# Where the first two output products of a merge are begun, and which banks a recurrence uses

## The chip, the cores and the metric

The kernel runs on one core of one Trainium2 chip. The metric is the device time of one execution in microseconds (us), the median of several runs. TensorE (PE in the rows) does the matrix products into PSUM, which has eight banks of 128 x 512 fp32 numbers; PEld is its weight load; VectorE is DVE, ScalarE is ACT, GpSimd is POOL, and SyncE (SP) issues the transfers from memory.

## The reference, cut to what matters

Two layers of a first block are computed, then two layers of a second block, on 512 tokens of width 1024, all in fp32. A layer of the first block is:

```python
proj = rmsnorm(x, norm_w[l]) @ w_in[l]          # q, k, v, gates, z and gate_a, gate_b
y_a = gated_delta_branch(q_a, k_a, v_a, ab_a, z_a, ...)     # 8 heads, both directions
y_b = diff_attention_branch(q_b, k_b, v_b, z_b, ...)        # 8 heads
merged = (jax.nn.sigmoid(gate_a) * (y_a @ w_pa[l])
          + jax.nn.sigmoid(gate_b) * (y_b @ w_pb[l]))
x = x + merged @ w_out[l]
```

The second block (window attention, gated attention, an mLSTM and a feed-forward part) isn't touched by the change.

## The kernel before, in words

Everything lies transposed in SBUF: a matrix of 512 tokens x 1024 is eight tiles (K-tiles) of 128 x 512. A product of one 128-column tile of a weight is eight K-steps, and each K-step is three matmuls of 128x128 by 128x512 (high part by high part, high by low, low by high; lines L309, L312, L313, in `Stream.product`), since each fp32 operand is split into two parts of the faster type fp32r. So a product is 24 matmuls into one bank.

A phase is a `Block`: all engines start it together and its end is a barrier. A layer runs delta_phase, merge_phase (a), diff_phase, merge_phase (b), out_phase. A merge has eight output tiles. Output tile n is `sigmoid(h @ gate tile) * (y @ weight tile)`, and its two products use the two halves of one weight chunk of 1 MB. The half 0 products (gates, from `hT`) go to banks 0 and 1, the half 1 products (outputs, from `yS`) to banks 2 and 3. The chunks (i, c), with i from 0 to 3 and c 0 or 1, are a `Stream`:

- `load` (L219) is issued on SP into `raw[c]`. SP issues chunk (i+1, c) when chunk (i, c) has been split (`load_after`, called from `run_sync`). The delta and diff phases issue the merge's chunks (0, 0) and (0, 1) themselves and no more: chunk (1, 0) and (1, 1) are the first thing that SP issues in the merge phase. In the second layer's merge (b), 832 KB of constants are issued on SP ahead of them (the argument `pairs`).
- `high` (ACT, L260) and then `low` (DVE, L266) split a chunk from `raw` into the slot `ws[c]`. Both wait for the load and for `slot_free`, which the first matmul of a product raises that was built with `frees`: when PE begins with one slot, the other is free.
- PE waits in `ready` for both parts.

The last head of delta and the last heads of diff have no further projections to compute. PE there takes work from a generator (`fill`, taken in pieces by `some(fill, n)` and emptied by `drain(fill)`). Its last part is `first_gates`: the two half 0 products of the merge's chunks (0, 0) and (0, 1). The merge phase then begins on PE with the two half 1 products of these chunks, 48 matmuls, and continues with chunk (1, 0).

In the last head of delta the recurrence over four chunks (s = 0 to 3) runs in two directions d: PE forms k by the state (`ks`, L1548, bank AB+d = 4 and 5), DVE forms r, PE forms y (L1555, bank YB+d = 6 and 7), ACT copies it out as v_new (L1730), PE forms the state's product (L1568, bank AB+d) and the outputs (L1579, L1581, bank 3). After s = 3 ACT squares the outputs (L1668), DVE normalises them (L1820), PE transposes them (`turn_out`, L1454), DVE gates them (L1825), ACT and DVE write the high and low parts of `yS` (L1677, L1831), and the phase ends. The end of diff has the same chain: PE forms the last output (L2126), ACT squares (L2190), DVE normalises (L2264), PE transposes (`turn_out`, L2097), DVE gates (L2273), ACT and DVE write the parts (L2197, L2279).

Of the kernel before, what the change touches and what calls it, by code (L numbers as in the profile page):

```python
# [10 lines left out]
ALU = mybir.AluOpType  # L11
# [3 lines left out]
P = 128  # L15
# [11 lines left out]
HEADS = 8  # L27
# [321 lines left out]
def whole(gen):  # L349
    for last in gen:  # L350
        pass
    return last
# [322 lines left out]
        yield  # L675


def first_outputs(k, pe, st, banks, x, steps, ready):

    st.credit(pe)  # L680
    st.ready(pe, 0, 0)
    halves = [st.product(pe, k.bank[banks[h]][:, :], 0, h, x, steps=steps, end=False) for h in range(2)]
    for t in steps:
        ready(t)
        for part in halves:
            next(part)
            yield


def merge_phase(k, st, following, yS, macc, mS, pairs=()):  # L690

    nc = k.nc
    st.open()
    tile, sig, mul, step, hi, loaded = k.sems("tile_ready", "sigmoid_ready", "merged_ready", "merge_step", "merged_high_done",
                                              "constants_loaded")
    with ExitStack() as ctx:
        room = Carve(k.cb[:, :], F32)
        sg, mt = room(2, SEQ), room(2, SEQ)

        with nc.Block() as block:  # L700
            @block.gpsimd
            def _(pool):
                k.clear_old(pool)

            @block.sync
            def _(sp):
                for dst, src in pairs:
                    sp.dma_start(dst, src).then_inc(loaded, 16)
                st.run_sync(sp, following)
                sp.wait_ge(loaded, 16 * len(pairs))  # L710

            @block.tensor
            def _(pe):
                pe.sem_inc(tile, 1)
                for c in range(2):
                    st.ready(pe, 0, c)
                    whole(st.product(pe, k.bank[2 + c][:, :], c, 1, yS, frees=c == 1)).then_inc(tile, 2 - c)

                with pe.Fori(1, KT // 2) as i:
                    for c in range(2):  # L720
                        st.ready(pe, i, c)

                        pe.wait_ge(mul, nth(i, 2, c))
                        whole(st.product(pe, k.bank[c][:, :], c, 0, k.hT)).then_inc(tile, 1)
                        whole(st.product(pe, k.bank[2 + c][:, :], c, 1, yS)).then_inc(tile, 1)
                if mS is not None:

                    pe.wait_ge(mul, 2 + KT - 1)
                    drain(first_outputs(k, pe, following, OUT_BANKS_MERGE, mS, MERGE_FIRST, lambda t: pe.wait_ge(mul, 3 + t)))

            @block.scalar
            def _(act):
                def body(i, c, last):
                    act.wait_ge(tile, nth(i, 4, 2 * c))
                    act.activation(sg[:, c], k.bank[c][:, :], ACT.Sigmoid).then_inc(sig, 1)
                    if mS is not None:
                        act.wait_ge(step, nth(i, 4, 2 * c + 1))
                        act.activation(mS[:, 0, bass.ds(i * 2 + c, 1)], mt[:, c:c + 1], ACT.Copy).then_inc(hi, 1)
                pipelined(act, KT // 2, 2, lambda i, c: st.high(act, i, c), body, lambda: following.first_high(act, st),
                          handed=True)  # L740
                if mS is not None:
                    following.second_high(act)

            @block.vector
            def _(dve):
                chain = Chain(dve, step)

                dve.sem_inc(mul, 2)

                def body(i, c, last):  # L750
                    n = i * 2 + c
                    dve.wait_ge(sig, nth(i, 2, c))
                    dve.wait_ge(tile, nth(i, 4, 2 * c + 1))
                    if mS is None:
                        dve.tensor_tensor(macc[:, bass.ds(n, 1)], sg[:, c:c + 1], k.bank[2 + c][:, :].rearrange("p (o n) -> p o n", o=1),
                                          ALU.mult).then_inc(mul, 1)
                    else:
                        chain.at(i, 4, 2 * c)
                        chain(dve.tensor_tensor(mt[:, c], sg[:, c], k.bank[2 + c][:, :], ALU.mult))
                        chain(dve.tensor_tensor(mt[:, c:c + 1], mt[:, c:c + 1], macc[:, bass.ds(n, 1)], ALU.add))  # L760
                        dve.wait_ge(hi, nth(i, 2, c))
                        dve.tensor_tensor(mS[:, 1, bass.ds(n, 1)], mt[:, c:c + 1], mS[:, 0, bass.ds(n, 1)].bitcast(F32),
                                          ALU.subtract).then_inc(mul, 1)
                pipelined(dve, KT // 2, 2, lambda i, c: st.low(dve, i, c), body, lambda: following.first_low(dve, st),
                          handed=True)
                if mS is not None:
                    following.second_low(dve)
                dve.wait_ge(mul, 2 + KT)
    k.next_phase()


OUT_BANKS_MERGE, OUT_BANKS_ATT = (0, 2, 1, 3), (0, 1, 2, 3)
MERGE_FIRST = tuple(range(KT - 1))

# [395 lines left out]
def delta_phase(k, st, following, l, pA, cg, tab, lam, yS, wsp):  # L1170
# [23 lines left out]
    with ExitStack() as ctx:  # L1194
# [74 lines left out]
        with nc.Block() as block:  # L1269
# [123 lines left out]
            def _(pe):  # L1393
# [22 lines left out]
                def gates_ahead():  # L1416

                    for x, step in enumerate(first_gates(k, pe, following, taken, 4 * HEADS)):
                        yield
                        if x == KT - 1:  # L1420
                            for _ in range(KT):
                                yield

                def scratch(name, core):
                    use = scratch_use(name, core)
# [71 lines left out]
                def core(i, p, first=False, ahead=2):  # L1497
# [41 lines left out]
                    for s in range(NS):  # L1539
# [11 lines left out]
                        for d in range(2):  # L1551
                            c = chunk(d, s)
                            if s > 0:
                                pe.wait_ge(r_ready, nth(i, 2 * (NS - 1), 2 * (s - 1) + d))
                            pe.matmul(B[YB + d][:, 0:P], Xf[:, d, c], tmv[:, c] if s == 0 else r[:, d], start=True, stop=True).then_inc(y_ready, 1)  # L1555
                        if s == 1 and ahead:
                            turn_k(i + 1, 1 - p, i)
                        if s == 2 and ahead:
# [26 lines left out]
                            some(fill, 2 if s == 2 else 1)  # L1585
                    if ahead:
                        gram(i + 1, 1 - p, q, YB)
                    drain(fill)

                st.ready(pe, 0, 0)  # L1590
                for last in first_chunk(st, pe, (B[0][:, :], B[1][:, :]), k.hT, norm.ready(pe), gates.product(pe)):
# [15 lines left out]
                gram(0, 0, kk[:, 0], YB + 1)  # L1607
                gram(0, 0, q, YB)
                cores(core)
                turn_out(HEADS - 1, HEADS - 1, "out")  # L1610

            @block.scalar
            def _(act):
# [69 lines left out]
                def core(i, p, first=False, ahead=2):  # L1683
# [42 lines left out]
                    for s in range(NS):  # L1726
                        for d in range(2):
                            c = d * NS + chunk(d, s)
                            act.wait_ge(y_ready, nth(i, 2 * NS, 2 * s + d))
                            act.activation(vn[:, d], B[YB + d][:, 0:P], ACT.Copy, scale=small(p, BP + c, 1)).then_inc(vn_ready, 1)  # L1730
                        if not ahead:
                            continue
                        if s == 0:
                            silu(i + 1, 1 - p, 1)
                        elif s == 1:
                            token_squares(i + 1, 1 - p, 1, i)
                            copy_k(i + 1, i)
                            if ahead > 1:
                                st.high(act, i + 2, 1)
                        elif s == 2:  # L1740
                            silu(i + 1, 1 - p, 2)
                            token_squares(i + 1, 1 - p, 0, i)
                            act.preload_act_table_set(LN_EXP)
                            if ahead > 1:
                                pad_copy(i + 2, 0)
# [239 lines left out]
def diff_phase(k, st, following, lam, yS):  # L1985
# [22 lines left out]
    with ExitStack() as ctx:  # L2008
# [17 lines left out]
        with nc.Block() as block:  # L2026
# [38 lines left out]
            def _(pe):  # L2065
                st.credit(pe)

                def stream():
# [12 lines left out]
                    for _ in first_gates(k, pe, following, taken, 4 * HEADS):  # L2081
                        yield
                        yield

                def turn_v(h):
                    pe.wait_ge(raw_ready, nth(h, 3, 2))
# [50 lines left out]
                for u in range(UNITS1):  # L2137
# [9 lines left out]
                        output(u - 1)  # L2147
                    some(fill, KT)
                output(UNITS1 - 1)
                drain(fill)  # L2150
                turn_out(HEADS - 1)

            @block.scalar
            def _(act):
# [952 lines left out]
def build(nc, a, out):  # L3107
    ctx = ExitStack()
    with ctx:
# [22 lines left out]
        with ExitStack() as one:  # L3132
# [10 lines left out]
            for l in range(DEPTH):  # L3143
# [3 lines left out]
                delta_phase(k, s_delta, s_ma, l, pA, cg, tab, lam, yS, split)  # L3147
                with ExitStack() as two:
                    macc = k.sb(two, "macc", [P, KT, SEQ], F32)
                    merge_phase(k, s_ma, s_diff, yS, macc, None)  # L3150
                    diff_phase(k, s_diff, s_mb, lam, yS)
                    with ExitStack() as three:
                        mS = k.sb(three, "mS", [P, 2, KT, SEQ], F32R)
                        merge_phase(k, s_mb, s_out, yS, macc, mS, () if more else [(k.cb[:, CB_CAUS:CB_N], a["cb"][:, CB_CAUS:CB_N])])
                        out_phase(k, s_out, s_next, mS, macc[:, 0:2], OUT_BANKS_MERGE, KT - 1, [(pA[:, :], a["pA"][l + 1])] if more else (),
                                  weights(split, a["gA"], l + 1) if more else None)
        with ExitStack() as one:
# [66 lines left out]
```

## Time and profile before

| what | us |
| --- | --- |
| median of 3 runs (3218.54 to 3222.21) | 3218.66 |
| the profiled execution, its own time | 3222.45 |
| its span in the profile | 3220.7 |
| PE busy, of the span | 3033.8 |
| end of delta's last DVE work to merge (a), first layer | 462.52 to 463.37 |
| end of diff's last DVE work to merge (b), first layer | 827.90 to 828.74 |

The profile times each instruction of one execution on each engine, from the span's start. A line of a timeline has the start, the duration, the engine, the source line, the operation with its output and inputs, a count if several are merged, and in brackets the idle time of the engine before it with what ended it. Matmuls overlap each other in the records, so the pace of a run of them is read from the distance of their starts.

### The profile page before, as it was taken

Reading aid. Unit: us, or ns where it says so; the run is one execution under the profiler, and the core shown is the slowest. Engines: PE = TensorE matmul, PEld = TensorE weight load, DVE = VectorE, ACT = ScalarE, POOL = GpSimd, SP = SyncE. Lnnn points to the kernel's source line nnn. Section 1 sums busy time; section 2 is a strip of 40 time slices with the busy share of each in tenths; the row PEclk is TensorE's granted clock in tenths of the full one; section 3 lists DMA queues with packets and bytes.
Section 4 is the critical chain, followed back from the end, with each engine's and each line's share of the span. In section 5 each row is a group of like instructions: output and inputs, shape, how many; then the busy total and the mean of one; then the engine's idle time right before and its main releaser. Section 6 shows DMA issues by size and latency. Waiting matters only on the chain. (4 is left out here: it accounts for less than half of the span.)

```text
span 3220.7 us, 55034 instructions
## 1 busy us (share of the span) xinstructions
PE 3033.8 (94%) x22250; PEld 2393.4 (74%) x22250; DVE 1701.3 (53%) x2532; ACT 1456.3 (45%) x2841; POOL 418.3 (13%) x276
## 2 busy tenths in 40 slices
PE   7999989999898999899999989989999999899998
PEld 4777767777776777777776867767888777678887
DVE  5777742566446777724665435544333445443343
ACT  4455532555334555523555245643333356543332
POOL 1544510000013455400000010001000100010000
PEclk9999999999999999999999999989999999999999
DMA  3211112221222112022221222112222221022222
GB/s 130 74 61 61 61 49 92 70 70 56 83 91 80 61 63 78 28 79 82 69 71 61 83 93 82 40 40 92 101 95 91 79 82 53 4 102 95 101 91 79
DMA packets 39723, 239.34 MB, mean 74 GB/s; under 512 B 6352, under 2 KB 6992, under 8 KB 13904
## 3 DMA queue, kind: packets, MB, share of 16 engines
q1 hardware_dynamic: 39504, 236.27, 21.4%
q8 instruction: 156, 2.56, 0.3%
q14 instruction: 63, 0.52, 0.1%
HBM read 229.36 MB, written 2.16 MB: 72 GB/s over the span
## 5 line engine op out<-in xcount | busy, mean ns | idle before, releaser
L309 PE MATMUL bank<-hT,ws 128*128 128x512 f32 x2112 | 877.4, 415 | 53.9 <-DVE hT L500 26.2
L313 PE MATMUL bank<-hT,ws 128*128 128x512 f32 x2112 | 831.5, 394 | 0.0
L312 PE MATMUL bank<-hT,ws 128*128 128x512 f32 x2112 | 830.4, 393 | 1.0 <-issue 1.0
L309 PEld LDWEIGHTS bank<-hT,ws 128*128 128x128 f32 x2112 | 400.9, 190 | 145.6 <-issue 66.2
L266 DVE TENSOR_TENSOR ws<-raw,ws 128x2048 fp32r<-128x2048 f32 x160 | 367.6, 2298 | 216.1 <-ACT ws L260 213.4
L260 ACT ACTIVATE ws<-raw 128x2048 fp32r<-128x2048 f32 x172 | 328.8, 1911 | 327.8 <-PE bank L309 204.5
L313 PEld LDWEIGHTS bank<-hT,ws 128*128 128x128 f32 x2112 | 399.6, 189 | 89.7 <-issue 1.6
L312 PEld LDWEIGHTS bank<-hT,ws 128*128 128x128 f32 x2112 | 401.9, 190 | 69.5 <-issue 1.4
L917 PE MATMUL bank<-uS,ws 128*128 128x512 f32 x512 | 201.8, 394 | 0.0
L921 PE MATMUL bank<-uS,ws 128*128 128x512 f32 x512 | 201.2, 393 | 0.0
L920 PE MATMUL bank<-uS,ws 128*128 128x512 f32 x512 | 200.3, 391 | 0.0
L1796 DVE SCALAR_TENSOR_TENSOR cb<-cb,cw 128x512 f32<-128x512 f32 x192 | 177.9, 927 | 4.7
L309 PE MATMUL bank<-yS,ws 128*128 128x512 f32 x384 | 160.0, 417 | 20.8 <-PEq L1269 6.2
L313 PE MATMUL bank<-yS,ws 128*128 128x512 f32 x384 | 157.8, 411 | 0.0
L312 PE MATMUL bank<-yS,ws 128*128 128x512 f32 x384 | 157.7, 411 | 0.0
L455 POOL TENSOR_TENSOR sq<-sq 128x512 f32<-128x512 f32 x18 | 35.1, 1950 | 926.6 <-ACT sq L444 926.6
L1000 DVE TENSOR_TENSOR uS<-u,uS 128x512 fp32r<-128x512 f32 x64 | 44.3, 693 | 206.4 <-ACT uS L983 206.4
L1004 DVE TENSOR_TENSOR xT<-xT,bank 128x512 f32<-128x512 f32 x128 | 87.9, 687 | 121.7 <-PE bank L921 121.1
L2184 ACT ACTIVATE pr<-bank,sc 128x512 f32<-128x512 f32 x128 | 86.6, 682 | 140.8 <-DVE sc L2250 140.8
L2250 DVE TENSOR_REDUCE sc<-bank 128x1 f32<-128x512 f32 x128 | 82.3, 685 | 119.2 <-PE bank L2108 119.2
L455 POOL TENSOR_TENSOR macc<-macc 128x512 f32<-128x512 f32 x12 | 25.3, 2106 | 787.1 <-ACT macc L444 787.1
L979 ACT ACTIVATE u<-bank 128x512 f32<-128x512 f32 x64 | 38.3, 599 | 181.1 <-PE bank L313 181.1
(361 smaller groups left out, 4903.7 us busy)
## 6 DMA issues: line engine op xcount, KB each, us to landing
raw<-in_w_ff SPq DMA_DIRECT2D x64, 1024.0 KB, 4.9
raw<-in_w_delta SPq DMA_DIRECT2D x32, 1024.0 KB, 4.9
raw<-in_w_diff SPq DMA_DIRECT2D x32, 1024.0 KB, 4.9
raw<-in_w_att SPq DMA_DIRECT2D x20, 1024.0 KB, 4.9
raw<-in_w_merge_a SPq DMA_DIRECT2D x16, 1024.0 KB, 4.9
raw<-in_w_merge_b SPq DMA_DIRECT2D x16, 1024.0 KB, 5.0
raw<-in_w_out SPq DMA_DIRECT2D x16, 1024.0 KB, 5.0
rows<-sum_rows SPq DMA_DIRECT2D x16, 512.0 KB, 6.1
```

The costliest lines, as they stand in the source:

```text
L260: act.activation(self.k.ws[:, c % 2, 0], self.k.raw[:, c % 2], ACT.Copy).then_inc(self.high_done, 1)
L266: dve.tensor_tensor(self.k.ws[:, c % 2, 1], self.k.raw[:, c % 2], self.k.ws[:, c % 2, 0].bitcast(F32), ALU.subtract).then_inc(self.low_don ...
L309: first = pe.matmul(out, hi, x[:, 0, k], start=(begin and k == steps[0]), stop=False)
L312: pe.matmul(out, hi, x[:, 1, k], start=False, stop=False)
L313: last = pe.matmul(out, lo, x[:, 0, k], start=False, stop=(end and k == steps[-1]))
L917: first = pe.matmul(o, hi, uS[:, 0, kk], start=(kk == 0), stop=False)
L920: pe.matmul(o, hi, uS[:, 1, kk], start=False, stop=False)
L921: last = pe.matmul(o, lo, uS[:, 0, kk], start=False, stop=(kk == 3))
L1004: dve.tensor_tensor(k.xT[:, n], k.xT[:, n], k.bank[4 + n % 4][:, :], ALU.add).then_inc(added, 1)
L1796: ins = dve.scalar_tensor_tensor(cv[:, j], pad[:, j, w:w + SEQ], cw[:, j, w:w + 1], cv[:, j], ALU.mult, ALU.add)
L2184: act.activation(pr[:, u % 2, m], B[SB + m][:, :], ACT.Exp, bias=sc[:, u % 2, m:m + 1], accum_out=sc[:, u % 2, 2 + m:3 + m]).then_inc(p_re ...
L2250: dve.tensor_reduce(sc[:, u % 2, m:m + 1], B[SB + m][:, :], AX_X, ALU.max, negate=True).then_inc(max_ready, 1)
```

## The change

Seven of the eight K-steps of each of the two half 1 products of chunks (0, 0) and (0, 1) are issued in the phase before, as the last part of the same generator (`first_merges`): in delta's last head into banks 6 and 7, in diff's into banks 4 and 5. The merge phase then issues the eighth K-step of each, three matmuls, and reads these banks for its first two output tiles. `frees` stays at the first matmul that the merge phase issues for chunk (0, 1). The transposes at the end of both phases are issued with steps of the generator ahead of them and behind them: four ahead and the rest behind in delta, six ahead and the rest behind in diff. The recurrence's product y moves, in all eight heads, from the first 128 columns of banks 6 and 7 to columns 256 to 383 of banks 4 and 5, whose first 128 columns hold `ks` and the state's product.

```diff
+def first_merges(k, pe, st, banks, x, ready):
+
+    halves = [st.product(pe, k.bank[b][:, :], c, 1, x, frees=False, steps=MERGE_FIRST, end=False) for c, b in enumerate(banks)]
+    for t in MERGE_FIRST:
+        ready(t)
+        for part in halves:
+            next(part)
+            yield
...
-def merge_phase(k, st, following, yS, macc, mS, pairs=()):
+def merge_phase(k, st, following, yS, macc, mS, begun, pairs=()):
...
-                    whole(st.product(pe, k.bank[2 + c][:, :], c, 1, yS, frees=c == 1)).then_inc(tile, 2 - c)
+                    whole(st.product(pe, k.bank[begun[c]][:, :], c, 1, yS, frees=c == 1, steps=(KT - 1,), begin=False)).then_inc(tile, 2 - c)
...
+                    merged = k.bank[begun[c] if isinstance(i, int) and i == 0 else 2 + c][:, :]
...
+MERGE_DELTA, MERGE_DIFF = (6, 7), (4, 5)
 OUT_BANKS_MERGE, OUT_BANKS_ATT = (0, 2, 1, 3), (0, 1, 2, 3)
 MERGE_FIRST = tuple(range(KT - 1))
...
+                    yield from first_merges(k, pe, following, MERGE_DELTA, yS, lambda t: pe.wait_ge(ylo_ready, t + 1))
...
-                            pe.matmul(B[YB + d][:, 0:P], Xf[:, d, c], tmv[:, c] if s == 0 else r[:, d], start=True, stop=True).then_inc(y_ready, 1)
+                            pe.matmul(B[AB + d][:, QUAD:QUAD + P], Xf[:, d, c], tmv[:, c] if s == 0 else r[:, d], start=True, stop=True).then_inc(y_ready, 1)
...
-                    drain(fill)
+                        drain(fill)
+                    else:
+                        some(fill, 4)
+                        turn_out(i, i, "out")
+                        drain(fill)
...
-                turn_out(HEADS - 1, HEADS - 1, "out")
...
-                            act.activation(vn[:, d], B[YB + d][:, 0:P], ACT.Copy, scale=small(p, BP + c, 1)).then_inc(vn_ready, 1)
+                            act.activation(vn[:, d], B[AB + d][:, QUAD:QUAD + P], ACT.Copy, scale=small(p, BP + c, 1)).then_inc(vn_ready, 1)
...
+                    pe.wait_ge(p_ready, 2 * UNITS1)
+                    yield from first_merges(k, pe, following, MERGE_DIFF, yS, lambda t: pe.wait_ge(ylo, t + 1))
...
                 output(UNITS1 - 1)
+                some(fill, 6)
+                turn_out(HEADS - 1)
                 drain(fill)
-                turn_out(HEADS - 1)
```

## Rows read from the trace of the kernel before

**Rows 1.** The page's part 1: busy time and share of the span.
```profile
PE 3033.8 (94%) x22250; PEld 2393.4 (74%) x22250; DVE 1701.3 (53%) x2532; ACT 1456.3 (45%) x2841; POOL 418.3 (13%) x276
```

**Rows 2.** Timeline of the end of diff, first layer.
```profile
821.00 1.05 PE L2126 MATMUL bank<-vtm,AT 128*128 128x128 f32 x8
...
825.01 0.66 PE L2097 MATMUL bank<-cc,O 128*128 128x128 f32 x4 [2.95 <-DVE O L2264]
...
827.21 0.69 DVE L2279 TENSOR_TENSOR yS<-yt,yS 128x512 fp32r<-128x512 f32 x1 [0.75 <-ACT yS L2197]
...
828.74 0.77 PE L309 MATMUL bank<-yS,ws 128*128 128x512 f32 x1 [3.07 <-PEq L2026]
```

**Rows 3.** Timeline of the end of delta, first layer, and SP's first issue in merge (a).
```profile
459.17 1.11 PE L1454 MATMUL bank<-cc,o 128*128 128x128 f32 x4 [2.63 <-DVE o L1820]
...
461.83 0.69 DVE L1831 TENSOR_TENSOR yS<-tmv,yS 128x512 fp32r<-128x512 f32 x1 [0.76 <-ACT yS L1677]
...
463.37 0.76 PE L309 MATMUL bank<-yS,ws 128*128 128x512 f32 x1 [3.09 <-PEq L1269]
...
463.86 1.95 SPq L219 DMA_DIRECT2D raw<-in_w_merge_a  x2
```

**Rows 4.** Busy time by stretch: PE's count and granted clock, PEclk (1.00 is 2.4 GHz).
```profile
463.30:467.70 4.40, 4.33 (x10) 3.47 (x11) 0.00 (x0) 1.62 (x2) 0.00 (x0) 0.50 0.68 214
467.70:472.00 4.30, 4.30 (x19) 3.46 (x18) 0.56 (x1) 0.34 (x1) 0.00 (x0) 0.96 0.71 269
822.00:825.00 3.00, 0.06 (x1) 0.00 (x0) 0.69 (x1) 1.98 (x10) 0.00 (x0) 1.00 0.00 0
```

**Rows 5.** Timeline of merge (a), first layer: how chunk (1, 0) becomes ready.
```profile
471.66 1.92 ACT L260 ACTIVATE ws<-raw 128x2048 fp32r<-128x2048 f32 x1 [6.72 <-PE bank L309]
...
473.71 2.29 DVE L266 TENSOR_TENSOR ws<-raw,ws 128x2048 fp32r<-128x2048 f32 x1 [1.58 <-ACT ws L260]
...
476.76 0.40 PE L309 MATMUL bank<-hT,ws 128*128 128x512 f32 x1
```

**Rows 6.** Timelines: PE begins chunk (1, 0) in the other three merges.
```profile
843.15 0.47 PE L309 MATMUL bank<-hT,ws 128*128 128x512 f32 x1 [0.92 <-issue]
...
1411.47 0.40 PE L309 MATMUL bank<-hT,ws 128*128 128x512 f32 x1
...
1778.36 0.47 PE L309 MATMUL bank<-hT,ws 128*128 128x512 f32 x1 [0.92 <-issue]
```

**Rows 7.** Timelines of SP: chunks (1, 0), (1, 1) issued in those three.
```profile
828.80 1.01 SPq L219 DMA_DIRECT2D raw<-in_w_merge_b  x2
...
1397.67 1.02 SPq L219 DMA_DIRECT2D raw<-in_w_merge_a  x2
...
1764.33 1.02 SPq L219 DMA_DIRECT2D raw<-in_w_merge_b  x2
```

**Rows 8.** DMA issues, chunk (1, 0) alone, four merges in time: us to landing.
```profile
raw<-in_w_merge_a SPq DMA_DIRECT2D x1, 1024.0 KB, 5.0
...
raw<-in_w_merge_b SPq DMA_DIRECT2D x1, 1024.0 KB, 5.1
...
raw<-in_w_merge_a SPq DMA_DIRECT2D x1, 1024.0 KB, 4.9
...
raw<-in_w_merge_b SPq DMA_DIRECT2D x1, 1024.0 KB, 6.2
```

**Rows 9.** Timeline of the recurrence: s = 0 with, s = 2 without a step between.
```profile
443.71 0.60 PE L1555 MATMUL bank<-tmv,Xf 128*128 128x128 f32 x4
...
444.85 0.60 PE L1568 MATMUL bank<-XT,kd 128*128 128x128 f32 x4
...
450.79 0.75 PE L1555 MATMUL bank<-XT,Xf 128*128 128x128 f32 x4 [0.29 <-DVE XT L1914]
...
451.74 0.75 PE L1568 MATMUL bank<-XT,kd 128*128 128x128 f32 x4 [0.20 <-ACT XT L1730]
```

More of the change, by code:

```diff
@@ L754, in body @@
                     if mS is None:
-                        dve.tensor_tensor(macc[:, bass.ds(n, 1)], sg[:, c:c + 1], k.bank[2 + c][:, :].rearrange("p (o n) -> p o n", o=1),
+                        dve.tensor_tensor(macc[:, bass.ds(n, 1)], sg[:, c:c + 1], merged.rearrange("p (o n) -> p o n", o=1),
                                           ALU.mult).then_inc(mul, 1)
@@ L758, in body @@
                         chain.at(i, 4, 2 * c)
-                        chain(dve.tensor_tensor(mt[:, c], sg[:, c], k.bank[2 + c][:, :], ALU.mult))
+                        chain(dve.tensor_tensor(mt[:, c], sg[:, c], merged, ALU.mult))
                         chain(dve.tensor_tensor(mt[:, c:c + 1], mt[:, c:c + 1], macc[:, bass.ds(n, 1)], ALU.add))
@@ L3149, in build @@
                     macc = k.sb(two, "macc", [P, KT, SEQ], F32)
-                    merge_phase(k, s_ma, s_diff, yS, macc, None)
+                    merge_phase(k, s_ma, s_diff, yS, macc, None, MERGE_DELTA)
                     diff_phase(k, s_diff, s_mb, lam, yS)
@@ L3153, in build @@
                         mS = k.sb(three, "mS", [P, 2, KT, SEQ], F32R)
-                        merge_phase(k, s_mb, s_out, yS, macc, mS, () if more else [(k.cb[:, CB_CAUS:CB_N], a["cb"][:, CB_CAUS:CB_N])])
+                        merge_phase(k, s_mb, s_out, yS, macc, mS, MERGE_DIFF, () if more else [(k.cb[:, CB_CAUS:CB_N], a["cb"][:, CB_CAUS:CB_N])])
                         out_phase(k, s_out, s_next, mS, macc[:, 0:2], OUT_BANKS_MERGE, KT - 1, [(pA[:, :], a["pA"][l + 1])] if more else (),
```

## Prediction, made before the change was run

> **What bounds the kernel.** The page comes first: PE is busy for 3033.8 us, 94% of the span [rows 1], and no other engine for more than 53%, so only PE's idle time, or PE's own work at a lower clock, can be saved. The timelines of the two kinds of phase end show where PE is idle. At the end of diff PE issues the last output at 821.00, is next busy at 825.01 after 2.95 us of idleness, and then idle for 3.07 us until the merge starts at 828.74 [rows 2]. At the end of delta it is idle for 2.63 us and for 3.09 us [rows 3]. There are four such ends (two layers), with some 6 us each. The view by stretches shows a second cost: the merge's first ten matmuls run in 4.4 us at a granted clock of 0.50 (1.2 GHz), the following nineteen in 4.3 us at 0.96 [rows 4]. So the reader sees two things that filling the end could save: idle time, and ten matmuls at 0.44 us in place of 0.23.
>
> The third thing to look at is what PE needs next. In merge (a) ACT begins to split chunk (1, 0) at 471.66, DVE at 473.71, and PE begins with the chunk at 476.76 [rows 5]. ACT had waited 6.72 us for a PE matmul, the one that frees the slot; the load had been issued at 463.86 [rows 3] and landed after 5.0 us [rows 8], at 468.9, and was hidden under the 48 matmuls. These are exactly the matmuls that the change takes away from behind it.
>
> **The moved matmuls.** Seven K-steps of two products are 14 steps, 42 matmuls. At 0.233 us each (nearest row: 19 in 4.30 us, 0.226, with clock 0.96 [rows 4]; the K-step of three is taken as 0.70 us) they are 9.8 us in each phase end. What is left in the merge is 6 matmuls, 1.4 us.
>
> **The end of delta.** By the order in the code, of the 14 steps one stands after the outputs of s = 1, two inside s = 2, two after it, two inside s = 3, four ahead of the transpose and three behind. Three stand where PE waits for nothing: 3 x 0.70 = 2.1 us on the chain. Those inside stand partly in waits: from y to the state's product it takes 1.14 us with a step between and 0.95 us without [rows 9], so 0.19 us; the same inside the pair of ks and y I put at 0.14, twice; the last stands in the wait for v_new and costs nothing. The outputs are late by 2.1 + 0.19 + 0.28 = 2.6 us. The four steps behind them, 2.8 us, cover ACT's squares and DVE's normalisation, which take about as long (PE's idle 2.63 us [rows 3]); if that cover were longer than the wait, each 0.1 us would be paid. The transpose gains: 1.11 us at the low clock [rows 3] against 0.66 us in diff [rows 2], 0.45 us. The three behind it, 2.1 us, end before the chain through DVE and ACT does (from 459.17 + 1.11 to 462.52, 2.2 us). So the merge starts 2.1 us later.
>
> **The end of diff.** The generator's calls count out so that four steps of `first_merges` stand ahead of the last output (L2126): 2.8 us. The output then issues for 0.9 us, six steps follow, 4.2 us, against a normalised output that comes 4.0 us after the output's start (821.00 to 825.01 [rows 2]): PE arrives 5.1 us after it, 1.1 us late. The transpose is thus at 825.01 + 3.9 = 828.9. Four steps behind it, 0.45 + 2.8 us, end at 832.2, DVE's last at 831.8 (2.9 us after the transpose, as 825.01 to 827.90). With PE last and its pipe to empty, and the 0.84 us from there to the merge, it starts at 833.1 instead of 828.74: 4.4 us later (bounds 3.9 and 4.6).
>
> **What is late next.** SP isn't changed: it issues chunk (1, 0) when the merge phase begins. PE has 1.4 us of work then. The chunk needs its landing, then 2.05 us from ACT's start to DVE's, 2.29 us of DVE [rows 5], and 0.1 us to PE: landing plus 4.45 us. For the second merges the order on ACT and DVE (first tile's sigmoid and sum ahead of the split) is done before the load lands, so it adds nothing. Queued behind PE's wait are all of the merge's remaining products, in order; ACT and DVE have nothing but this chunk. With SP's times [rows 3, 7], shifted by the start's delay, and the landings of the same transfers [rows 8]:
>
> - merge (a), layer 1: 463.86 + 2.1 + 5.0 + 4.45 = 475.4, before 476.76 [rows 5]: 1.35 earlier.
> - merge (a), layer 2: 1397.67 + 2.1 + 4.9 + 4.45 = 1409.1, before 1411.47 [rows 6]: 2.35 earlier.
> - merge (b), layer 1: 828.80 + 4.4 + 5.1 + 4.45 = 842.75, before 843.15 [rows 6]: 0.4 earlier.
> - merge (b), layer 2: 1764.33 + 4.4 + 6.2 + 4.45 = 1779.4, before 1778.36 [rows 6]: 1.0 later (here the constants are in front).
>
> Together 3.1 us are gained. The waits are about 8 us in each merge: the 48 matmuls filled the time of a load, and what the change saves in the phase end it gives back there.
>
> **The clock after that wait.** The merge's start in rows 4 shows what PE's idleness of 3.07 to 3.09 us after little work does: clock 0.50 for ten matmuls, 4.4 us. A wait of 8 us after six matmuls should do no less. Ten to twelve matmuls of chunk (1, 0) at 0.427 instead of 0.23 us cost 1.95 to 2.35 us, taken as 2.15, in each of four merges: 8.6 us. This replaces the low clock at the merge's start, whose end is already in the comparison. The Trainium skill ("TensorE: Matmul & The Clock Gate", section "HAM oscillation — how this bites in real kernels") describes this pattern: bursts of matmuls with a longer wait for a transfer between them each start at the low clock again. By that rule the change pays 8.6 us; if the trace's exception counted (822 to 825, 3 us nearly without work at clock 1.00 [rows 4]) it would pay nothing.
>
> **The moved banks.** The product y goes to the bank of ks and the state's product. In program order each of these is read before the other is written, by the same semaphores as before, so no wait is added. There are 128 products y (eight heads, four s, two d, two layers). The rows show the products to the one bank and to the other at the same 0.60 us when nothing is waited for [rows 9], equal within the 0.01 us of the record; so the bound is 128 x 0.01 = 1.3 us either way, and I take zero. The new waits in `first_merges` (low parts of heads 0 to 6, last exponentials) are fulfilled when PE arrives.
>
> **The sum.** -3.1 + 8.6 = +5.5 us. Against the profiled execution's own 3222.45 (span 3220.7 and 1.75 around it) that is 3228.0; this execution lies 3.8 us above the median of 3218.66, and the forecast for the median is 3224.2. A measurement of this kernel tells about 0.2% (6.4 us) from no change, so this is "no change", on the slow side of it.
>
> **Rivals.**
>
> *The load lands later.* Its price is the landing, one to one, as it ends the wait. Rows 8 show 4.9 to 6.2 us. Were all at 6.2, three merges lose 1.2 + 1.1 + 1.3 = 3.6 us more: +9.1, 3227.8, slower. It decides from 0.3 us more in each of three merges. For it: in the changed kernel two loads of 1 MB are issued in the same way, and the fourth landing shows how much it varies. Against it: three of four agree within 0.2 us. Chance 0.2.
>
> *The clock stays high through the wait.* Then -3.1 us, 3215.6, no change. For it the three microseconds at 1.00 [rows 4], against it the length of the wait. Chance 0.1.
>
> *The load is hidden anyway.* If chunk (1, 0) were there when PE wants it, the merges would go from their start to chunk (1, 0) in 1.4 us instead of 13.4 to 14.4 us: 12.0 to 13.0 less 2.1 or 4.4 of delay, near 9.9, 8.6, 10.3 and 8.6 us, about -37 us, 3181, faster. It needs SP to issue that load before the phase; the code and rows 3 and 7 have it at the start each time. Chance 0.07, for what I have overlooked.
>
> *The forecast*, with its own range 3220 to 3228: 0.63.
>
> **Chances.** Faster by over 0.2%: the hidden load and a remainder, 0.10. Slower: the later load, 0.2, and the upper third of the forecast's own range, 0.2: 0.40. Within 0.2%: 0.50. The range for 8 in 10 is 3215 to 3232: from the clock that stays high to a later load with twelve slow matmuls each; the hidden load stays outside.
>
> **What the changed profile would show.** Merge starts later by 2.1 and 4.4 us after the last output or recurrence step of the phase before; PE's two idle gaps at the phase ends gone, but for the barrier's 0.8 to 1 us; six matmuls of `yS` at 0.23 us at the merge's start; then 7 to 8.5 us of idleness that DVE's L266 ends, with ACT's L260 released by a DMA instead of a matmul; then some ten matmuls at 0.43 us. Wrong would be a wait under 5 us, matmuls at full pace behind it, or a start of the merge that moved by under 1 or over 6 us.

## The result, and the profile after

| kernel | median, us | executions | ratio to before | 95% interval |
| --- | --- | --- | --- | --- |
| before, beside it | 3218.54 | 13 | 1 | |
| changed | 3226.36 (3221.11 to 3232.26) | 13 | 1.0026 | 1.0019 to 1.0033 |
| changed, once more, beside a before of 3219.79 | 3226.93 | 11 | 1.0019 | 1.0010 to 1.0028 |

The changed kernel is 8.4 us slower by the first ratio (0.0026 x 3218.5; interval 6.1 to 10.6 us) and 6.1 us by the second (3.2 to 9.0 us), where 5.5 us slower was forecast. The forecast had set 0.2% as the bound of "no change" and gave "no change" a chance of 0.50, "slower" 0.40. The first ratio lies a little beyond that bound, the second just within it.

The profiled execution of the changed kernel is the fastest of its 13 (3221.11 us, span 3219.3), so its span says little by itself; its stages do. The changed kernel has other line numbers: there L1467 and L2115 are the transposes that were L1454 and L2097, and L2144 is the last output of diff, before L2126. First the start of merge (a) of the first layer, timeline of PE and ACT, with the lines that answer to [rows 3, 5]. This execution runs 1.92 us ahead of the profile of before at that point (SP issues its last chunk ahead of it at 368.33 instead of 370.25).

```profile
460.14 0.66 PE L1467 MATMUL bank<-cc,o 128*128 128x128 f32 x4
...
463.88 0.47 PE L309 MATMUL bank<-yS,ws 128*128 128x512 f32 x1 [0.99 <-PEq L1281]
...
469.35 1.91 ACT L260 ACTIVATE ws<-raw 128x2048 fp32r<-128x2048 f32 x1 [3.91 <-DMA raw<-in_w_merge_a]
...
471.40 2.29 DVE L266 TENSOR_TENSOR ws<-raw,ws 128x2048 fp32r<-128x2048 f32 x1 [5.24 <-ACT ws L260]
...
473.79 0.77 PE L309 MATMUL bank<-hT,ws 128*128 128x512 f32 x1 [8.27 <-DVE ws L266]
474.36 0.63 PE L312 MATMUL bank<-hT,ws 128*128 128x512 f32 x1
```

The reader is to see four things. The two idle gaps of [rows 3] are gone: the transpose has no idle time in front and takes 0.66 us instead of 1.11, and the merge starts after 0.99 us of idleness instead of 3.09. In their place PE is idle for 8.27 us before chunk (1, 0), and what ended it is DVE's part of the split. And ACT's idle time before that split was ended by a DMA, where it was a matmul in [rows 5]. Last, PE's records are then 0.63 us long and 0.42 us apart: the low clock. The view by stretches of the same kernel gives it in numbers (columns as in [rows 4]):

```profile
463.90:465.50 1.60, 1.60 (x6) 1.00 (x6) 0.03 (x1) 1.53 (x2) 0.00 (x0) 1.00 0.36 51
465.50:473.70 8.20, 0.02 (x1) 0.00 (x0) 2.96 (x3) 2.40 (x2) 0.00 (x0) 0.78 0.63 247
473.70:476.90 3.20, 3.11 (x7) 2.48 (x8) 0.88 (x2) 1.91 (x1) 0.00 (x0) 0.50 0.49 148
476.90:481.00 4.10, 4.10 (x19) 3.39 (x18) 2.00 (x1) 0.00 (x0) 0.00 (x0) 0.99 0.54 176
```

Six matmuls at clock 1.00, a wait in which the clock falls, seven at 0.50, then full speed. The other three merges, timeline of PE, which answer to [rows 6]:

```profile
840.88 0.77 PE L309 MATMUL bank<-hT,ws 128*128 128x512 f32 x1 [7.73 <-DVE ws L266]
...
1405.39 0.77 PE L309 MATMUL bank<-hT,ws 128*128 128x512 f32 x1 [7.71 <-DVE ws L266]
...
1775.05 0.77 PE L309 MATMUL bank<-hT,ws 128*128 128x512 f32 x1 [9.68 <-DVE ws L266]
```

PE's waits sum to a line that the kernel before doesn't have:

```profile
PE bank L309 <- DVE ws L266: 33.4, 4, 9.7
```

The end of diff, first layer (this execution is 1.36 us ahead there), answers to [rows 2]:

```profile
822.42 1.05 PE L2144 MATMUL bank<-vtm,AT 128*128 128x128 f32 x8
...
827.51 0.60 PE L2115 MATMUL bank<-cc,O 128*128 128x128 f32 x4
...
831.51 0.48 PE L309 MATMUL bank<-yS,ws 128*128 128x512 f32 x1 [0.59 <-PEq L2042]
```

Less the 1.36 us, the last output is 2.78 us later than before, the transpose 3.86, the merge's start 4.13.

### The profile page after: what moved, and what is told of

Same layout as the page of the kernel before. It is cut to its first block and busy times, and to the rows that moved or that the text cites. A ratio compares the mean times of both kernels' runs of the same rounds, so it can differ in the third digit from the quotient of the medians.

```text
span 3219.3 us, 55036 instructions
## 1 busy us (share of the span) xinstructions
PE 3024.6 (94%) x22250; PEld 2386.5 (74%) x22250; DVE 1703.6 (53%) x2532; ACT 1456.5 (45%) x2841; POOL 417.2 (13%) x276
## 5 line engine op out<-in xcount | busy, mean ns | idle before, releaser
L309 PE MATMUL bank<-hT,ws 128*128 128x512 f32 x2112 | 880.3, 417 | 85.5 <-DVE ws L266 33.4
L309 PEld LDWEIGHTS bank<-hT,ws 128*128 128x128 f32 x2112 | 402.4, 191 | 178.5 <-issue 98.5
L266 DVE TENSOR_TENSOR ws<-raw,ws 128x2048 fp32r<-128x2048 f32 x160 | 367.7, 2298 | 229.2 <-ACT ws L260 226.6
L309 PE MATMUL bank<-yS,ws 128*128 128x512 f32 x384 | 157.6, 410 | 11.5 <-issue 4.4
L312 PE MATMUL bank<-yS,ws 128*128 128x512 f32 x384 | 154.5, 402 | 0.0
L313 PE MATMUL bank<-yS,ws 128*128 128x512 f32 x384 | 154.4, 402 | 0.0
```

Of the source, the lines that this page charges most:

```text
L266: dve.tensor_tensor(self.k.ws[:, c % 2, 1], self.k.raw[:, c % 2], self.k.ws[:, c % 2, 0].bitcast(F32), ALU.subtract).then_inc(self.low_don ...
L309: first = pe.matmul(out, hi, x[:, 0, k], start=(begin and k == steps[0]), stop=False)
L312: pe.matmul(out, hi, x[:, 1, k], start=False, stop=False)
L313: last = pe.matmul(out, lo, x[:, 0, k], start=False, stop=(end and k == steps[-1]))
```

## The experiments

Each experiment is compared with executions of the kernel before on the same chip. The intervals are those of the ratio, and "us on before" is the ratio less one, times the median of before. It differs from the difference of the two medians by up to 1.5 us, and by 3.4 us for e10. e7, e10 and e11 have five executions each, the others 11 or 12.

One number more is used, the "four merges". In a profile, take the distance from a mark in or ahead of the last head of the phase before a merge to a mark at the next phase's start, less the same distance in the profile of before, and add up the four. The marks are ACT's table loads at 396.12 and 566.54, 801.93 and 970.90, 1329.10 and 1501.68, 1737.12 and 1894.05 us of before. This sum leaves out what wanders elsewhere, but it is one execution each. For the changed kernel it is +0.56, +1.33, -1.88 and +3.74, together +3.75, and +4.21 in its second profile. Three kernels that have all 48 matmuls in each merge, as before, give +1.93 (e1), +1.91 (e6) and +1.56 (e12). So the profile of before is itself about 1.8 us on the quick side there, and 1.8 us are to be taken off each of these sums.

**The moved banks alone (e1).**

```diff
-pe.matmul(B[YB + d][:, 0:P], Xf[:, d, c], ...)
+pe.matmul(B[AB + d][:, QUAD:QUAD + P], Xf[:, d, c], ...)
-act.activation(vn[:, d], B[YB + d][:, 0:P], ...)
+act.activation(vn[:, d], B[AB + d][:, QUAD:QUAD + P], ...)
```

> The kernel before, with nothing of the change but the recurrence's product y in banks 4 and 5. Theory (the moved banks cost nothing): the time of before, 3218.5 us, within 2 us. Rival (the shared bank costs something, spread over 16 heads): part of the 8 us that the change lost shows up here, 2 to 8 us slower.

Measured: 3220.79 us, ratio 1.0000 (0.9991 to 1.0008). The moved banks cost nothing that can be measured: zero, with 2.9 us either way.

**One phase end alone (e2, e3).** Only the steps of one phase are begun early; the other merge issues its two products whole, in banks 2 and 3.

```diff
-MERGE_DELTA, MERGE_DIFF = (6, 7), (4, 5)
+MERGE_DELTA, MERGE_DIFF = (6, 7), (2, 3)        # e2; e3: (2, 3), (4, 5)
-                    yield from first_merges(k, pe, following, MERGE_DIFF, yS, ...)     # e2; e3: the one in delta
```

> The change without its part in diff: merge (b) begins as before. Theory: two of four waits are left. The start of chunk (1, 0) is 1.35 and 2.35 us earlier, two stretches at the low clock cost 4.3 us: +0.6 us on before. Rival (the loss sits in the end of delta, or in the moved banks): most of +8 us.

> The change without the K-steps in delta: merge (a) begins as before; y's banks stay moved. Theory: -0.4 and +1.0 us for the start of chunk (1, 0), 4.3 us for the clock: +4.9 us on before. Rival (loss in delta): no difference from before.

Measured: e2 3220.60 us, ratio 1.0001 (0.9992 to 1.0009), +0.3 us; e3 3223.05 us, ratio 1.0011 (1.0002 to 1.0019), +3.5 us. The expectations were +0.6 and +4.9. By the ratios the diff part carries the larger loss, as the sum had it, but the two intervals overlap, and the four merges of the two profiles (+5.44 and +4.69) have it the other way round. So which end costs more isn't settled; e2's interval ends at +2.9 us, so the end of delta alone doesn't carry the loss. The two add to 3.8 us, 2 to 5 us short of what the whole shows; the intervals are wide enough for that. Where the steps of a phase stay in place, the merge behind it begins with 7 to 13 slow matmuls as before, and where they are moved, a wait of 7.7 to 9.4 us with 7 to 12 slow matmuls behind it appears.

**The clock in the wait (e4, e8).** Extra matmuls, results unused, keep PE at work in the wait.

```diff
+                for _ in range(DUMMIES):            # 30 in e4, 36 in e8
+                    pe.matmul(k.bank[4 if mS is None else 6][:, :], k.hT[:, 0, 0, 0:P], k.hT[:, 0, 0], start=True, stop=True)
+
                 with pe.Fori(1, KT // 2) as i:
```

> The changed kernel with 30 extra matmuls (128x128 by 128x512, results unused, in a free bank) between the two last K-steps and chunk (1, 0) of each merge, 7 us of work inside a wait of 7.7 to 9.7 us. Theory (the clock that falls in the wait costs 2.15 us in each merge): the waits stay, the matmuls behind them run at 0.23 us each, and the time falls by 8.6 us against the changed kernel's 3226.4, to about 3218. Rival (the loss is in the wait and the clock plays no part): no difference from the changed kernel, 3226.

> As the run with 30 extra matmuls, with 36 (8.4 us of work), which left 1.3 to 2.8 us of idleness and the clock high in two merges of four. Theory: the clock stays high in all four, the start of chunk (1, 0) moves by under 0.3 us: 7 to 8.6 us faster than the changed kernel, at most 1 us from before. Rival: as with 30, +3.5 us on before.

With 30, the timeline of PE shows the clock kept in the first two merges and lost in the two others, where the remaining idle time was longest (in the third after one matmul at full pace; its load landed after 6.5 us, where it took 4.8 in the changed kernel). The starts of chunk (1, 0), and in the last two a record behind it:

```profile
474.04 0.47 PE L309 MATMUL bank<-hT,ws 128*128 128x512 f32 x1 [1.32 <-issue]
...
840.44 0.47 PE L309 MATMUL bank<-hT,ws 128*128 128x512 f32 x1 [1.69 <-issue]
...
1405.44 0.47 PE L309 MATMUL bank<-hT,ws 128*128 128x512 f32 x1 [2.52 <-issue]
...
1406.11 0.63 PE L313 MATMUL bank<-hT,ws 128*128 128x512 f32 x1
...
1774.81 0.76 PE L309 MATMUL bank<-hT,ws 128*128 128x512 f32 x1 [2.79 <-issue]
1775.37 0.63 PE L312 MATMUL bank<-hT,ws 128*128 128x512 f32 x1
```

It measured 3222.37 us, ratio 1.0011 (1.0002 to 1.0020): +3.5 us on before, where the expectation had all four merges at full speed and the time of before. With 36, no matmul of chunk (1, 0) is slow in any merge. Its starts:

```profile
477.20 0.47 PE L309 MATMUL bank<-hT,ws 128*128 128x512 f32 x1
...
843.09 0.40 PE L309 MATMUL bank<-hT,ws 128*128 128x512 f32 x1
...
1407.52 0.47 PE L309 MATMUL bank<-hT,ws 128*128 128x512 f32 x1 [0.86 <-issue]
...
1775.79 0.47 PE L309 MATMUL bank<-hT,ws 128*128 128x512 f32 x1 [1.66 <-issue]
```

In the first layer's merge (a), which starts at 467.28 here, the view of stretches has the extra matmuls and the start of chunk (1, 0) at clock 1.00:

```profile
464.00:474.00 10.00, 9.01 (x41) 7.09 (x39) 2.13 (x3) 3.76 (x4) 0.00 (x0) 1.00 0.50 191
474.00:478.00 4.00, 3.91 (x18) 2.95 (x17) 2.89 (x2) 1.45 (x3) 0.00 (x0) 1.00 0.12 49
```

It measured 3219.04 us, ratio 0.9997 (0.9988 to 1.0006): 1.0 us faster than before. Against the changed kernel's +8.4 and +6.1 us that is 9.4 and 7.1 us, where 8.6 was forecast. By the four merges it is less: -0.52 against +3.75 and +4.21, so 4.3 and 4.7 us. Of the difference 1.3 us is known. In the third merge the load of chunk (1, 0) landed after 6.2 us instead of 4.8, and the chunk began 10.7 us after the merge's start instead of 9.4, a start that had been expected to move by under 0.3 us; in the other three it moved by 0.0 to 0.3.

So more matmuls, with nothing else altered, take the loss away. The clock is its cause, and without it the change is worth about nothing (-1.0 us, with 2.9 us either way): the idle time of the phase end is only moved.

**The load earlier (e5, e6).** SP issues the chunks (1, 0) and (1, 1) as its last work in the phase before. In the first layer that is far ahead: at 415.07 us in e5, where the merge starts at 462.89. e5 is the changed kernel with it, e6 and e12 (the same kernel again) the kernel before.

```diff
+    def second_loads(self, sp):
+        for c in range(2):
+            self.load_after(sp, 0, c)
...
-            with sp.Fori(0, self.N - 1) as i:
+            with sp.Fori(done, self.N - 1) as i:           # done = 1 in the merges
...
+                following.second_loads(sp)                 # last on SP in delta and in diff
```

> The changed kernel with the loads of the merge's chunks (1, 0) and (1, 1) issued by SP at the end of the phase before (as soon as (0, 0) and (0, 1) are split) instead of at the merge's start. Theory (the wait is for this load, then for the split): the landing falls out of the wait. Merge (a): the split starts when the slot is free, 0.8 us after the start, and chunk (1, 0) begins near 5.2 us after it instead of 9.9 and 9.4; merge (b): ACT is busy with the first tile until 3.7 us, so near 8.0 instead of 9.4 and 11.3. Sum -13.5 us against the changed kernel, so 5 us faster than before; the low clock is still paid in most merges. Rival (the wait is for something else, slot or banks): no difference from the changed kernel.

> The kernel before with the same earlier loads, nothing else. Theory: before, the load was hidden under 48 matmuls and the slot was what ACT waited for, so no difference, within 2 us. Rival (the load mattered already): faster by over 3 us.

> The kernel before with the earlier loads, once more: it came out 5.5 us slower than before, where no difference was expected, with no stage of its profile slower where the loads moved. If that was the spread between groups of executions: within 3 us of before. If the earlier loads cost something real: again 4 us or more.

In e5 the wait shrinks as the load leaves it. Timeline of PE, first layer (the kernels with earlier loads have five lines more ahead of these, so L314 and L271 are L309 and L266):

```profile
462.89 0.47 PE L314 MATMUL bank<-yS,ws 128*128 128x512 f32 x1 [0.99 <-PEq L1286]
...
468.77 0.61 PE L314 MATMUL bank<-hT,ws 128*128 128x512 f32 x1 [4.24 <-DVE ws L271]
...
836.19 0.77 PE L314 MATMUL bank<-hT,ws 128*128 128x512 f32 x1 [6.36 <-DVE ws L271]
```

Chunk (1, 0) of merge (a) begins 5.9 us after the start instead of 9.9 (5.2 had been expected: ACT began the split only 1.45 us after the start, at 464.34, behind its first sigmoid). Merge (b) begins it after 8.0 us, as expected. So the load was what PE waited for. The four starts of the chunk come 12.2 us earlier in sum, of 13.5 expected. It measured 3218.88 us, ratio 0.9993 (0.9984 to 1.0002), -2.3 us on before: 8 to 11 us better than the changed kernel. The low clock is still paid: behind the waits of 4.2 and 6.4 us there are 8, 11, 7 and 14 slow matmuls, no fewer than in the changed kernel.

e6 missed: 3224.70 us, ratio 1.0017 (1.0008 to 1.0026), +5.5 us where zero was expected. e12 was to tell chance from cost and speaks for a cost: 3223.29 us, ratio 1.0013 (1.0003 to 1.0024), +4.2 us. It isn't in the four merges of their profiles (+1.91 and +1.56, as in e1). Where it goes isn't settled: e6's profile is level with that of before at 1894 us, and its 2.2 us of longer span lie behind that, where nothing was changed. Something of 4 us that the earlier loads cost may also lie in e5, e7 and e11.

**Fewer steps moved (e7, e10, e11).** Only the first of the two products is begun early, 21 matmuls, and its steps stand where PE waits anyway: none ahead of diff's last output, none behind the outputs of s = 1 and s = 2 in delta. The merge keeps 27 matmuls to hide the split behind. e7 has the earlier loads, e10 hasn't, e11 is e7 with three K-steps of the second product more in delta, one ahead of the transpose and two behind it.

```diff
-    halves = [st.product(pe, k.bank[b][:, :], c, 1, x, frees=False, steps=MERGE_FIRST, end=False) for c, b in enumerate(banks)]
+    part = st.product(pe, k.bank[banks[0]][:, :], 0, 1, x, frees=False, steps=MERGE_FIRST, end=False)
...
-                    whole(st.product(pe, k.bank[begun[c]][:, :], c, 1, yS, frees=c == 1, steps=(KT - 1,), begin=False)).then_inc(tile, 2 - c)
+                    left = (KT - 1,) if c == 0 else tuple(range(KT))
+                    whole(st.product(pe, k.bank[begun[c]][:, :], c, 1, yS, frees=c == 1, steps=left, begin=c == 1)).then_inc(tile, 2 - c)
...
-                some(fill, 6)
+                some(fill, 4)
                 turn_out(HEADS - 1)
```

> Only the first of the two products is begun in the phase before (7 K-steps, 4.9 us), put where PE waits anyway (two inside s = 2, two inside s = 3 and three ahead of the transpose in delta; four ahead and three behind it in diff, none ahead of the last output), with the earlier loads. The merge keeps 27 matmuls, 6.3 us, with the slot free after 0.7 us. Theory: chunk (1, 0) is ready 5.2 us (a) and 8.0 us (b) after the start, so PE waits 0 and 1.7 us, the clock stays high, the start moves by less than 0.5 us: 7.1 and 6.4 us saved in each merge, 27 us faster than before. Rival (saving at the phase end is always given back): within 6 us of before.

> As the run that begins only the first product, but with the loads at the merge's start as in before. Theory (the wait is the load's): chunk (1, 0) is ready 9.5 us after the start, PE's 27 matmuls take 6.3 us (8.7 with a low clock at the start), so it waits 1 to 3 us; against before the start of chunk (1, 0) is 4 us earlier in (a), 3.4 to 4.7 us in (b): 12 to 16 us faster than before, less up to 4 us where the clock falls. It tells how much of the 18 us of that run was the earlier load.

> As the run that begins only the first product with earlier loads, and in delta three K-steps of the second product more, issued behind the transpose. There that run left 3.2 us of idleness at the end of delta and began the merge with 13 slow matmuls. Theory: the gap shrinks to 1.1 us, the merge starts at the high clock, 18 matmuls are left there, and chunk (1, 0) begins 5.2 us after the start instead of 9.0: 3.8 us less in each of two merges, 7.6 us, so 25 us faster than before. Rival (the split is ready later, or the clock falls all the same): within 3 us of that run.

| run | median, us | ratio (95% interval) | us on before | by the medians | expected | four merges |
| --- | --- | --- | --- | --- | --- | --- |
| e10 | 3210.31 | 0.9960 (0.9946 to 0.9973) | -12.9 | -9.5 | -12 to -16, less up to 4 | -6.4 |
| e7 | 3203.55 | 0.9944 (0.9930 to 0.9958) | -18.0 | -16.5 | -27 | -16.6 |
| e11 | 3198.11 | 0.9933 (0.9919 to 0.9946) | -21.6 | -21.7 | -25 | -25.1 |

All three beat both kernels, with the same idea and half to seven tenths of the steps. e10 shows that fewer steps gain without the earlier loads too. The order among the three is that of the medians, but the intervals of neighbours overlap. e10's four waits ahead of chunk (1, 0) are 2.0 to 4.5 us, with slow matmuls behind three of them. In e7 the miss is in merge (a): PE is idle for 3.18 us ahead of it in the first layer, as in before, and its first 13 matmuls run at 0.50 (in the second layer 3.07 us and seven):

```profile
462.00:465.80 3.80, 0.66 (x4) 0.42 (x4) 1.44 (x2) 1.00 (x2) 0.00 (x0) 0.87 0.00 0
465.80:471.50 5.70, 5.64 (x13) 4.46 (x14) 2.14 (x2) 3.91 (x4) 0.00 (x0) 0.50 0.00 1
```

In e11 the same place has 1.69 us of idleness and no low clock, and chunk (1, 0) begins 5.9 us after the start:

```profile
462.34 0.47 PE L314 MATMUL bank<-yS,ws 128*128 128x512 f32 x1 [1.69 <-PEq L1296]
...
468.23 0.47 PE L314 MATMUL bank<-hT,ws 128*128 128x512 f32 x1 [1.46 <-issue]
```

The step from e7 to e11 is 3.6 us by the ratios and 8.5 by the four merges, against 7.6 expected. By the times alone it isn't clear of noise; that the gap, the low clock and the later start of chunk (1, 0) are gone, in both layers, is what the traces show.

**The changed kernel once more (e9).**

> The changed kernel as it is, once more, for a second profile and a second ratio. Theory: +5.5 us on before by the sum of the terms, up to +8 as first measured; the four waits before chunk (1, 0) at 7.7 to 9.7 us with 7 to 13 slow matmuls behind each. Rival (the first ratio was a lucky or unlucky draw): within 2 us of before.

Measured: ratio 1.0019, as in the table at the top. Its waits are 8.31, 7.73, 7.86 and 9.74 us (33.6 in sum, 33.4 in the first profile), with 7, 10, 10 and 6 slow matmuls of chunk (1, 0) behind them, against 7, 10, 7 and 13 in the first. The waits repeat; how long the clock stays down behind them repeats in the first layer only.

## Why the prediction was right, step by step

*The moved matmuls.* Right: six at the high clock in 1.6 us where the merge began with ten at the low one.

*The end of delta.* Forecast 2.1 us later; measured 463.88 against 463.37 less 1.92, 2.43 us. In the second layer the start came only 0.8 us later in the first profile. That is under the 1 us which the prediction had named as a sign of being wrong. But the profile of before has a stretch at the low clock in that last head (granted clock 0.86 between 1330 and 1355 us, 1.00 in the changed one's same stretch), and in e9, whose last head is as slow as in before, the start comes 2.1 us later. So the 0.8 is luck of that execution, no gain of the change.

*The end of diff.* Forecast 2.8, 3.9 and 4.4 us for output, transpose and merge; measured 2.78, 3.86 and 4.13.

*What is late next.* Right. Landings 5.0 and 6.4 us in the first and the last merge, and 4.44 us from ACT's start to PE's in the first (469.35 to 473.79), forecast 4.45. With the profiles' offsets, chunk (1, 0) begins 1.05, 0.91 and 3.70 us earlier and 1.00 us later; forecast 1.35, 0.4 and 2.35 earlier and 1.0 later. The sum is 4.7 us instead of 3.1, 1.3 us of it the low clock in before's last head just named; in e9 it is 3.1 to 3.2. The last wait, 9.7 us, is longer than the 7 to 8.5 that the prediction named, though its own sum for that merge gives 9.7 (1779.4 less the start at 1768.3, less 1.4).

*The clock.* Forecast ten to twelve slow matmuls and 2.15 us for each merge, 8.6 us. The two profiles have 6 to 13 in a merge; the sums, 37 and 33, give 7.2 and 6.4 us at 0.195 each, and the two ratios beside e8's 9.4 and 7.1. The mechanism is shown by e8, not only argued; that the size came out so near is in part luck, since the counts vary by a factor of two. Behind all eight waits of 7.7 to 9.7 us in two profiles the clock was low. The rule of the Trainium skill cited there (page "TensorE: Matmul & The Clock Gate", section on HAM oscillation) agrees.

*The moved banks.* Forecast zero, measured zero (e1).

*The sum.* +5.5 forecast, +8.4 and +6.1 measured: the forecast lies just below the first interval and inside the second. What is left over is 1 to 3 us. By parts, the first profile gives -4.7 + 7.2 = +2.5, or +3.75 for the four merges; of that, 1.8 us also stand in kernels whose merges are as before (e1, e6, e12), which leaves 2.0 us for the change. So the profiles of single executions show 4 to 6 us less of a loss than the ratios do, and don't show where the rest lies. The executions that they come from are part of it: the first profile of the changed kernel is 5.3 us below its median and the second 2.4, the one of before 3.8 us above its own. e6 and e12 have a loss that their profiles don't show either, so it stays open with them.

*The rivals.* The later load didn't come in the changed kernel (4.8 to 5.0 us in three merges of both profiles, 4.9 to 5.1 before), though it is no rare thing: see the last section. The clock that stays high is ruled out, and e4 and e8 show what it would have given. The hidden load didn't come by itself, and e5 shows that it isn't enough either: the split behind it still takes 4.3 us and 6 matmuls hide 1.4 of them.

## What to carry to other kernels

Before work is moved ahead of a boundary to fill idle time there, look at what hides behind it where it is now: here 48 matmuls covered the load and split of the next weights, and with 6 left the idle time came back behind the boundary, four waits of 8 to 10 us. Move only as much as fills the gap, and put it where PE waits anyway: 21 matmuls alone gained 9 to 13 us here where 42 lost 6 to 8. Then let the next load start earlier as well: 21 to 30 matmuls with that gained 18 to 22 us, though the earlier loads by themselves cost 4 to 6 us for a reason that isn't known. A long wait of PE costs its length and then the slow matmuls behind it.

## What the runs showed of the hardware

The granted clock goes with the spread here. Of the changed kernel's 13 executions the fastest (3221.11 us) has a mean granted clock of 0.982 and one of the three slowest (3231.62 us) 0.975, and in every one of the kernels the slower executions tend to have the lower clock. Which of the two comes first these numbers don't tell. One place of it is seen: in the last head of delta PE is at work in short pieces for some 24 us in which the clock is 1.00 in the profile of before and 0.79 in e7's, of kernels that issue the same work there, and the stretch is 2.4 us longer with it.

How long an idle gap may be before the clock falls can't be read off as one number. Gaps of 0.99, 1.32, 1.46, 1.69 and 2.03 us (e10) were followed by full speed. One of 2.52 us (e4) was followed by one matmul at full pace and then the low clock, though 36 matmuls at full rate stood ahead of it. One of 2.95 us in before was followed by four transposes at clock 1.00 (0.66 us [rows 2]). And in e10 a gap of 3.09 us ahead of merge (a), where before has ten slow matmuls behind 3.09 us, was followed by five matmuls at full pace before the clock fell:

```profile
465.43 0.47 PE L309 MATMUL bank<-yS,ws 128*128 128x512 f32 x1 [3.09 <-PEq L1286]
...
466.45 0.45 PE L312 MATMUL bank<-yS,ws 128*128 128x512 f32 x1
466.70 0.63 PE L313 MATMUL bank<-yS,ws 128*128 128x512 f32 x1
```

So the fall can come behind the gap, not only in it. All twelve waits of 4.2 us and more in the changed kernel's two profiles and in e5's had the low clock behind them.

Last, a load of 1 MB issued with a second behind it landed in 4.8 to 5.3 us in most merges. In merge (b) of the second layer, behind 832 KB of constants, it took 6.1 to 7.2 us. The constants aren't the only cause of such a landing: without any ahead of it, merge (a) has 6.8 us in e1 and, in the second layer, 6.2 in e3, 6.5 in e4, 6.2 in e8 and 6.1 in e10. What makes these late isn't known.
